# A transformer trunk on one core: cross attentions reordered head by head, expert outputs combined through a 0/1 matrix in two rounded halves, the router's stretch reordered, and 60 extra transposes on TensorE

## What is computed

```
def memory_cross_attention(h, mem_n, wq, wkv, wo):          # 4 heads of 256
    s = einsum('blhd,bmhd->bhlm', q, k) * 256 ** -0.5
    o = einsum('bhlm,bmhd->blhd', softmax(s), v)
    return o @ wo

def moe_swiglu(h, router_w, w_gate, w_up, w_down):
    top_v, top_i = lax.top_k(t @ router_w, 2)
    gates = sum(one_hot(top_i, 8) * softmax(top_v)[..., None], axis=1)
    for e in range(8):
        out = out + gates[:, e:e + 1] * swiglu(t, w_gate[e], w_up[e], w_down[e])
```

## Time and profile before

| | |
|---|---|
| runs | 1725.4, 1728.24, 1728.98 us |
| the profiled execution's own time | 1726.68 us |
| its span, first to last instruction | 1724.9 us |
| TensorE busy | 1673.4 us (97%) |
| VectorE, ScalarE, GpSimd busy | 1297.6 us, 1039.2 us, 21.0 us |
| mean granted TensorE clock | 0.985 of full speed |
| read from HBM | 459.7 MB, 267 GB/s over the span |
| expert passes, 716 to 1718 us | 8 |

### The profile page before, as it was taken

The page is one execution under the profiler, slowest core; times in us unless marked ns, Lnnn a source line. Parts: engine busy times, 40 slices in busy tenths (PEclk is TensorE's granted clock), DMA queues, the critical chain, the costliest instruction groups (busy, mean ns, idle before and its releaser), DMA issues.

```text
span 1724.9 us, 23270 instructions
## 1 busy us (share of the span) xinstructions
PE 1673.4 (97%) x8662; PEld 1419.5 (82%) x8662; DVE 1297.6 (75%) x1120; ACT 1039.2 (60%) x935; POOL 21.0 (1%) x32
## 2 busy tenths in 40 slices
PE   6999999999999999699999999999999999999997
PEld 5997879999887797688888888888788788788785
DVE  6783645555467764698888888888888988988886
ACT  5341435444356544577677677677677677677674
POOL 1000000000000100000000000000000000000000
PEclk9996999999999999899999999999999999999999
DMA  8651525655654445499899899999879999999992
GB/s 314 200 190 50 176 93 171 196 174 192 195 172 137 132 147 198 150 369 370 323 365 372 315 380 359 322 370 372 324 277 365 325 366 349 340 375 342 346 371 120
DMA packets 222435, 461.44 MB, mean 268 GB/s; under 512 B 7314, under 2 KB 52580, under 8 KB 222388
## 3 DMA queue, kind: packets, MB, share of 16 engines
q1 hardware_dynamic: 221696, 459.53, 75.0%
q0 software_dynamic: 528, 1.22, 0.2%
q10 hardware_dynamic: 164, 0.04, 0.0%
HBM read 459.72 MB, written 1.05 MB: 267 GB/s over the span
## 4 chain that ended last, share of the span: by engine, by line
issue 60%; PE 35%; DVE 3%; ACT 1%; DMA 0%; POOL 0%; ACTq 0%; DVEq 0%; POOLq 0%
PE ps L1518 14%; PE ps L1504 8%; PE ps L1743 4%; PE ps L1666 3%; PE ps L1627 1%; PE ps L1594 1%; PE ps L1613 1%; PE ps L1584 1%; DVE w_lo L368 1%; PE ps L1692 0%; ACT w_hi L364 0%; ACT a_hi L542 0%; DMA rows<-in_ev_conv_w 0%; DVE a_lo L879 0%; DVE u L1035 0%
## 5 line engine op out<-in xcount | busy, mean ns | idle before, releaser
L368 DVE TENSOR_TENSOR w_lo<-raw,w_hi 128x2048 fp32r<-128x2048 f32 x431 | 981.8, 2290 | 248.2 <-ACT w_hi L364 246.8
L364 ACT ACTIVATE w_hi<-raw 128x2048 fp32r<-128x2048 f32 x431 | 826.8, 1919 | 364.5 <-PE ps L1893 138.1
L1893 PE MATMUL ps<-w_hi,e_hi 128*128 128x512 f32 x896 | 354.2, 395 | 3.1 <-DVE e_lo L1369 3.1
L1893 PE MATMUL ps<-w_hi,e_lo 128*128 128x512 f32 x896 | 349.6, 390 | 0.0
L1893 PE MATMUL ps<-w_lo,e_hi 128*128 128x512 f32 x896 | 349.0, 389 | 0.0
L1893 PEld LDWEIGHTS ps<-w_hi,e_hi 128*128 128x128 f32 x896 | 168.3, 188 | 36.5 <-issue 3.3
L1893 PEld LDWEIGHTS ps<-w_hi,e_lo 128*128 128x128 f32 x896 | 168.2, 188 | 35.8
L1893 PEld LDWEIGHTS ps<-w_lo,e_hi 128*128 128x128 f32 x896 | 168.4, 188 | 33.6
L1915 PE MATMUL ps<-w_hi,at_hi 128*128 128x512 f32 x448 | 175.0, 391 | 1.9 <-DVE at_lo L1381 1.9
L1915 PE MATMUL ps<-w_hi,at_lo 128*128 128x512 f32 x448 | 174.4, 389 | 0.0
L1915 PE MATMUL ps<-w_lo,at_hi 128*128 128x512 f32 x448 | 174.3, 389 | 0.0
(11 more groups left out here) (294 smaller groups left out, 1816.0 us busy)
## 6 DMA issues: line engine op xcount, KB each, us to landing
raw<-in_moe_w_up SPq DMA_DIRECT2D x112, 1024.0 KB, 6.9
raw<-in_moe_w_gate SPq DMA_DIRECT2D x110, 1024.0 KB, 7.0
raw<-in_moe_w_down SPq DMA_DIRECT2D x110, 1024.0 KB, 6.1
raw<-in_xa_wkv SPq DMA_DIRECT2D x16, 1024.0 KB, 5.1
raw<-in_ev_w_in SPq DMA_DIRECT2D x14, 1024.0 KB, 8.7
raw<-in_od_w_in SPq DMA_DIRECT2D x12, 1024.0 KB, 5.0
raw<-in_ffd_w_gate SPq DMA_DIRECT2D x11, 1024.0 KB, 5.4
raw<-in_ffd_w_up SPq DMA_DIRECT2D x11, 1024.0 KB, 5.3
```

The source lines that it names most:

```text
L364: nc.scalar.activation(w_hi[:, n % CUT, :], at_, ACT.Copy).then_inc(hi_cut, 1)
L368: nc.vector.tensor_tensor(w_lo[:, n % CUT, :], place(n, r, behind)[0], w_hi[:, n % CUT, :].bitcast(F32), ALU.subtract).then_inc(lo_cut, 1)
L1893: mm = T.matmul(ps[:, bank, :], s, m, start=(h == 0 and k == 0 and j == 0), stop=(h == 1 and k == 3 and j == 2))
```

## The change

Four parts.

1. **Cross attentions by heads.** The scores, the transposes and the values of a head are put between the slabs of wq and wo. wo is taken with both column halves of its upper rows first, then of its lower rows, so that its first slabs need only heads 0 and 1. The banks are by kind: scores in 4 and 5 by turns, transposes in 6, values in 7. ACT and DVE get their order written out, slab cuts in between.
2. **0/1 combine.** `spread` is the transpose of `pack` itself, float32r. y is written as `y_hi` (ACT) and `y_lo` (DVE), both float32r, and `combine` is two matmuls for each of the four pieces. The gate is multiplied in where DVE adds to X. `pgate` goes.
3. **The router's stretch.** Some slab cuts, the calculation of the gates, the load of ACT's Silu table and the waits for the table of passes change places; the opening of the first pass is taken out in front of the loop. The entries behind 8 of the table are made with 5 operations in place of 11.
4. **60 transposes** of the identity into PSUM bank 3: 4 after the router's product, 24 before the counting matmuls, 20 before the gather, 12 after it.

```
-            slabs[f"o{i}"] = t_all(kpn(xa_wo[i]))
+            slabs[f"o{i}"] = [t_slab(kpn(xa_wo[i]), 512 * b)[h] for h in range(2) for b in range(2)]
 # ACT, cross
-                stage(f"q{i}", 4)
-                for h in range(XH): (exp of each head)
-                for h in range(XH): (xa_pt of each head)
-                for h in range(XH): (a_hi of each head)
-                stage(f"o{i}", 4 if i == 0 else 3)
+                cut(0) ; cut(1) ; cut(2) ; exps(0) ; cut(3) ; turned(0) ; exps(1) ; head_hi(0) ; turned(1)
+                exps(2) ; head_hi(1) ; exps(3) ; cut(4) ; turned(2) ; head_hi(2) ; turned(3) ; cut(5)
+                head_hi(3) ; cut(6)
+                if i == 0:
+                    cut(7)
 # DVE, cross
+                cut(0) ; q_got(0) ; cut(1) ; q_got(1) ; top(0) ; cut(2) ; shares(0) ; q_got(2) ; top(1)
+                cut(3) ; shares(1) ; q_got(3) ; head_lo(0) ; top(2) ; top(3) ; shares(2) ; head_lo(1)
+                shares(3) ; cut(4) ; head_lo(2) ; cut(5) ; head_lo(3) ; cut(6)
+                dve.wait_ge(slab_used, FIRST[f"o{i}"] + 3)
+                x_event(0, f"o{i}")()
 # TensorE, cross
+                q_slab(0) ; q_slab(1) ; scores(0) ; q_slab(2) ; scores(1) ; turn_p(0) ; q_slab(3)
+                values(0) ; scores(2) ; turn_p(1) ; scores(3) ; values(1)
+                o_slab(0, 0, {2: lambda: turn_p(2)})
+                values(2) ; turn_p(3)
+                o_slab(1, 0, {2: lambda: values(3)})
+                o_slab(0, 1, {})
+                o_slab(1, 1, {2: lambda: turn_x(0)} if i == 1 else {})
 # ACT, router and passes
+            cut_hi(act, G0 + 1)
             for h in range(2):
                 act.wait_ge(acc_free, BANKS["o1"] + 2 * h + 2)
...
-            cut_hi(act, G0 + 1)
+            cut_hi(act, G0 + 2)
             act.wait_ge(n_rstd, NORMS["moe"] + 1)
...
-            cut_hi(act, G0 + 2)
             act.wait_ge(r_m, 1)
             nc.scalar.activation(lg[:, 9, 2:4], lg[:, 9, 0:2], ACT.Exp).then_inc(r_e, 1)
-            act.wait_ge(r_tab, 1)
-            n_pass = act.value_load(table[0:1, 0:1], min_val=NE, max_val=NE + 3)
             nc.scalar.activation(mx[:, 0:1], ident[:, 0:1], ACT.Silu).then_inc(g_sig, 1)
...
+            def y_up(q):
+                act.wait_ge(slab_used, G0 + PASS + PASS * q)
+                nc.scalar.activation(y_hi[:, :], ps[:, 2:4, :].rearrange("p a n -> p (a n)"),
+                                     ACT.Copy).then_inc(y_top, 1)
 # a_next: cut G0, pack_hi, cut G0+1, y_up(q - 1), then cuts G0+2 to G0+5
 # DVE, router and passes
-            stage("o1", 3, {1: x_event(0, "o1"), 2: lambda: turn_lo("moe", a_hi, a_lo, tiles=range(4))})
+            cut_lo(dve, G0 + 1)
+            turn_lo("moe", a_hi, a_lo, tiles=range(4))
...
-            cut_lo(dve, G0 + 1)
             dve.wait_ge(r_lt, 1)
             V.tensor_copy(logits[:, :], ps[0:NE, LOGITS, 0:256]).then_inc(r_ls, 1)
...
             V.tensor_tensor(mask, one1, one2, ALU.add).then_inc(r_cnt, 1)
+            cut_lo(dve, G0 + 2)
             dve.wait_ge(r_ps, 2)
 # the gates (L1317 to L1325 before) now come behind pack_lo(0) and the cuts of G0+3 to G0+5
             def v_y(q):
-                dve.wait_ge(slab_used, G0 + PASS + PASS * q)
-                V.tensor_copy(y[:, :], ps[:, 2:4, :]...).then_inc(y_sb, 1)
+                dve.wait_ge(y_top, q + 1)
+                V.tensor_tensor(y_lo[:, :], ps[:, 2:4, :]..., y_hi[:, :]..., ALU.subtract).then_inc(y_sb, 1)
 # add_pass
-                    V.tensor_tensor(X[:, t, :], ps[...], X[:, t, :], ALU.add)
+                    V.scalar_tensor_tensor(out=X[:, t, :], in0=ps[...], scalar=gate16[:, t, bass.ds(col, 1)],
+                                           in1=X[:, t, :], op0=ALU.mult, op1=ALU.add)
 # TensorE, router and passes
+            def keep_going(n):
+                for _ in range(n):
+                    T.transpose(ps[:, 3, 0:P], ident, ident)
+            keep_going(4)
             pe.wait_ge(r_ls, 1)
...
+            keep_going(24)
             pe.wait_ge(r_cnt, 1)
...
+            keep_going(20)
...
-                        mm = T.matmul(ps[:, b0 + o, :], spread[:, t * P:(t + 1) * P], y[:, 512 * o:512 * o + 512],
-                                      start=True, stop=True)
+                        for yv in (y_hi, y_lo):
+                            mm = T.matmul(ps[:, b0 + o, :], spread[:, t * P:(t + 1) * P],
+                                          yv[:, 512 * o:512 * o + 512], start=yv is y_hi, stop=yv is y_lo)
...
             gather(0)
+            keep_going(12)
+            opening(0)
             pe.wait_ge(r_tab, 1)
```

More of the change, by code:

```diff
@@ L150, in trunk_kernel @@
         ta = sb("ta", [P, 2048])
+        with ExitStack() as s:
+            sb("tb_front", [P, D], F32, s)
+            y_lo = sb("y_lo", [P, D], F32R, s)
         tb = sb("tb", [P, 2048])
@@ L820, in a_next @@
                 pack_hi(q)
-                for n in range(1, 6):
+                cut_hi(act, G0 + 1, 7 * q, behind)
+                y_up(q - 1)
+                for n in range(2, 6):
                     cut_hi(act, G0 + n, 7 * q, behind)
@@ L1343, in _ @@
             pack_tokens(0)
-            over, incl, rk, hit = (row16[:, i, 0:8] for i in range(4))
+            over, incl, rk = (row16[:, i, 0:8] for i in range(3))
             link(V.tensor_scalar(over, ps[0:1, 1, 16:24], float(BLK), None, ALU.is_gt))
@@ L1484, in room, with slab_t, gemm_t @@
                     pe.wait_ge(acc_free, upto - 4)
-            def gemm_t(name, blocks, hi, lo, base=None, before_last=None):
+            def slab_t(n, bank, h, hi, lo, before_k=None):
+                slab_ready(n)
+                wh, wl = (shaped(w[:, n % CUT, :], 4) for w in (w_hi, w_lo))
+                for k in range(4):
+                    if before_k is not None:
+                        before_k(k)
+                    for t in range(2):
+                        ah, al = (a[:, 4 * h + k, t * P:(t + 1) * P] for a in (hi, lo))
+                        for j, (s, m) in enumerate(cuts(ah, al, wh[:, k, :], wl[:, k, :])):
+                            mm = T.matmul(ps[:, (bank + t) % 4, :], s, m, start=(h == 0 and k == 0 and j == 0),
+                                          stop=(h == 1 and k == 3 and j == 2))
+                mm.then_inc(slab_used, 1)
+            def gemm_t(name, blocks, hi, lo, base=None):
                 for b in range(blocks):
@@ new lines, in cross @@
+                q_slab(0)
+                q_slab(1)
+                scores(0)
+                q_slab(2)
+                scores(1)
+                turn_p(0)
+                q_slab(3)
+                values(0)
+                scores(2)
+                turn_p(1)
+                scores(3)
+                values(1)
+                o_slab(0, 0, {2: lambda: turn_p(2)})
+                values(2)
+                turn_p(3)
+                o_slab(1, 0, {2: lambda: values(3)})
+                o_slab(0, 1, {})
@@ L1932, in _, with opening @@
             gather(0)
-            pe.wait_ge(r_tab, 1)
-            n_pass = pe.value_load(table[0:1, 0:1], min_val=NE, max_val=NE + 3)
-            with pe.Fori(0, n_pass) as q:
+            def opening(q):
                 pe.wait_ge(e_l, q + 1)
@@ L1943, in _ @@
                 half_in(G0 + 3, i, 1, 1)
+            keep_going(12)
+            opening(0)
+            pe.wait_ge(r_tab, 1)
+            n_pass = pe.value_load(table[0:1, 0:1], min_val=NE, max_val=NE + 3)
+            with pe.Fori(0, n_pass) as q:
                 with pe.If(q > 0):
+                    opening(q)
                     combine(q - 1)
-                pe.wait_ge(pg_rdy, q + 1)
                 for t in range(2):
-                    mm = T.transpose(ps[:, 5, t * P:(t + 1) * P], pgate[:, t, :], ident)
+                    mm = T.transpose(ps[:, 5, t * P:(t + 1) * P], pack[:, t, :], ident)
                 mm.then_inc(pg_ps, 1)
```

196 lines of the change are left out of this document (123 added, 73 removed).

## The result

Before: 1727.51 us, median of 4 runs (1725.4 to 1728.98). Changed: **1708.32 us**, median of 4 (1707.91 to 1708.48). Ratio 0.9889, 95% interval 0.9872 to 0.9907. The profiled execution of the changed kernel has an own time of 1708.24 us and a span of 1706.4, so 18.5 us of span less than the one of before.

| stretch of the span | before, us | after, us | difference | forecast |
|---|---|---|---|---|
| start to wq of cross attention 0 | 202.77 | 204.46 | +1.7 | 0 |
| wq to the end of wo, cross attention 0 | 66.8 | 60.9 | -5.9 | -5.2 |
| between | 353.6 | 353.6 | 0 | 0 |
| wq to the router's product, cross attention 1 | 67.3 | 68.4 | +1.1 | +2.4 |
| router's product to G0 | 25.7 | 19.0 | -6.7 | -5.6 |

The account below looks back on a forecast made before the run. TensorE was taken to bound the kernel, its instructions setting each expert pass. Cross attention 0 -5.2, cross attention 1 with the router's stretch -3.2 and passes -9.1 sum to -17.5 us: forecast 1709.5 us, range 1702 to 1718.

Parts of the forecast that it names:

- Cross attention 0: From wq to the end of wo: softmax beside slabs removes 5.8 us of waits and half clock, less 0.6: -5.2 us.
- ten changes between kinds of matmul: In cross attention 0: some ten more switches between matmul kinds may cost 0.1 us each, 0.6 taken.
- Cross attention 1: Late G0 load leaves 5.3 us idle in wo's last slab, eating the gain: +0.4, plus +2 for half clock.
- Router's stretch: From wo's end to the first matmul of G0: reordered cuts, full-clock gather, transposes and earlier Silu table load: -5.6 us.
- The 20 transposes: Before the gather: they take 2.1 us where TensorE waited 1.8 for `pack`: +0.3 us.
- beside the counting: 0: Router's stretch: DVE's 2.3 us cut of G0+2 runs beside the counting's five pairs, costing 0.
- Passes: Expert passes: seven at -1.4 us each, first pass +0.8 to 1, end -0.3; together -9.1 us.
- The wait at G0+6 of the first pass: First expert pass: the gates' seven operations ahead of DVE's cut, less `pgate`, cost +0.8 to 1 us.
- The first rival: Router's stretch: transposes don't hold the clock, so it falls during the wait for the pick: 1713 us, chance 0.25.
- G0 isn't what wo waits for: Cross attention 1: values 3 or loads come earlier, so it gains 5.3 us without half clock: 1702 us, chance 0.1.
- Cuts fall behind in every pass: Expert passes: y's chain through ACT and DVE makes TensorE wait 1 us, not 0.2: 1715 us, chance 0.12.
- The ring of loads runs dry: Expert passes: loads limit; at 340 GB/s a pass takes 129.5 us: 1755 us total, chance 0.03.

Follow-up runs that it names:

- experiment 1: Changed kernel with the loads of G0 to G0+3 issued before the wait for values 3 of cross attention 1: 1700.12 us.
- experiment 2: Changed kernel with VectorE's first addition to X put ahead of its cut of G0 in cross attention 1: 1706.21 us.
- experiment 11: The kernel of experiment 9 without any of the change's 60 transposes: 1688.29 us.
- experiment 5: Changed kernel with the gates' seven operations moved on VectorE ahead of the cuts of G0+3 to G0+5: 1706.64 us.
- experiment 3: Changed kernel without its 60 transposes of the identity: 1709.87 us.
- experiment 4: Changed kernel with 42 more transposes of the identity ahead of turn_x(0) in cross attention 1, G0's load still late: 1705.89 us.
- experiment 9: Changed kernel with G0's loads early, gates early, and added transposes ahead of mem's turn, in the retention and ahead of the last combine: 1684.9 us.
- experiment 6: Changed kernel with the old float32 combine: y copied by VectorE, one float32 matmul per half bank: 1718.63 us.
- experiment 12: Kernel before with only the two cross attentions by heads, wo's new slab order and their cuts, softmax and additions: 1724.93 us.
- experiment 7: Changed kernel with 13 more transposes of the identity in the retention, ahead of the first head's values: 1695.92 us.
- experiment 10: The kernel of experiment 9 with the change's 60 transposes cut down to the 24 ahead of the counting: 1688.63 us.
- experiment 8: Changed kernel with G0's loads early, gates early, 13 transposes ahead of mem's turn and 18 ahead of the last combine: 1699.4 us, one execution 1685.13.

## Why the prediction was right, point by point

- **Total.** 1709.5 forecast, 1708.3 measured. The parts of the change made 20.2 us where 17.5 were counted; the profile's start gave 1.7 back. The two errors are opposed, so that the sum came within 1.2 us is partly luck. (Added up straight, the ends of the parts give 1705.5 to 1715.7, not 1706 to 1714.)
- **Cross attention 0**, -5.2 against -5.9: right in mechanism. The 0.6 for ten changes between kinds of matmul was the mis-sized term: they cost nothing, the chain adds up from 1.73, 0.44 and the slabs.
- **Cross attention 1**, +2.4 against +1.1. Its idle time was forecast at 5.3 us with the chain that it has, and measured at 5.14; experiment 1 shows the cause, experiment 2 that the chain's last link was not it. The half clock behind it was forecast at 2 us; 68.4 less 61.6 less 5.1 leaves 1.7. The largest part of the difference is again the changes between kinds of matmul, 0.8 us here, which cost nothing: values 3 end 47.3 us behind wq's start instead of 47.9, and the load goes out with them.
- **Router's stretch**, -5.6 against -6.7. From the router's product to the logits' copy 9.3 us became 5.6: -3.7 (forecast -3.4). From there to the gather 7.7 became 7.2: -0.5, where +0.3 was forecast. Two terms were mis-sized. The 20 transposes were priced against a wait of 1.8 us, but `pack` itself is ready at 700.05, 0.1 us ahead of their end: +0.1 and not +0.3. And "beside the counting: 0" left out what full clock is worth there: from the first counting matmul to the gather it is 3.53 us, 3.82 in experiment 11, where all five pairs run at half clock (0.43 us apart instead of 0.22), and 4.07 before. The last 0.2 is a wait of 0.22 us that DVE had inside the calculation of `pack` and has no longer. From gather to G0 8.7 became 6.2: -2.5, as forecast.
- **Passes**, -9.1 against -8.7. Combine -1.6, as forecast. The wait at G0+2 forecast at 0.2 is 0.1 or less, so a pass gained 1.5, not 1.4. The wait at G0+6 of the first pass was forecast at 0.8 to 1 and is 1.34, from the gates' operations (experiment 5). The end was forecast at -0.3 and came out at +0.1: TensorE waits 2.37 us for `y_lo` and the clock falls within the last combine (0.63 us for its last matmuls), which the prediction did not look for.
- **The first rival**, that transposes don't hold the clock, falls. It was drawn from the fall around 236 us, where groups of four transposes stand between waits, and held back by a wait of 3 us seeming too short against one of 4.22. Both readings were wrong. Ahead of those transposes stood a wait of 1.70 us (to 234.81), and in the changed kernel the same groups of four stand in cross attention 0 without a wait and without a fall. The wait of 2.92 us is enough for a fall (experiment 3), and the transposes prevent it. The clock stayed at 1.00 through 24 and 20 transposes in the router's stretch, fell without them (experiments 3 and 11), and stayed through 42 in a row (experiment 4). The Trainium skill (TensorE: Matmul & The Clock Gate, Part 4: PE-mode transpose) says that full clock does not engage for transposes, since they don't count as busy in the same way. For these ones (float32, 128x128 by the identity) the trace disagrees, and the measurement decides. That they also raise a clock at half is read from durations alone: the first 16 transposes of the kernel, behind two tiny matmuls, take 3.34 us in the changed kernel and 3.65 before, so the last ones were faster.
- **G0 isn't what wo waits for**: it was (experiment 1). **Cuts fall behind in every pass**: no wait at G0+2 or G0+6 after the first pass. **The ring of loads runs dry**: DMA share 0.98 at 357 GB/s, no wait for a load. With the version of experiment 9, whose passes have the same length, the same holds.

What decides whether the clock falls at 33 us is settled in part by the length of the wait. Ten profiles are of kernels without transposes ahead of the turn of mem. In four of them (the kernel before, experiments 1, 2 and 3) the first slab starts at half speed (0.63 us a matmul until 21 to 22 us), the wait is 1.3 to 1.5 us, and the clock stays. In the other six the first slab is at full speed and the wait is 3.1 us; four of these fall (the changed kernel, experiments 4, 6 and 12), two do not (5 and 7). What decides between these, and behind the waits of 1.5 to 1.9 us elsewhere, stays open: the retention's 1.5 us brought the clock down in nine of ten profiles, the 1.9 us for `at_lo` in two of fourteen (experiments 2 and 4). That the four timed runs of the changed kernel all fell at 33 us, as their spread of 0.6 us, their equal mean clock of 0.987 and experiment 1 suggest, is argued, not shown.

## What to carry to other kernels

A reordering that closes one wait brings the next one forward: follow the first load behind the reordered stretch to the wait that holds its issue, for it was late before and nobody asked for it. Read the granted clock over the whole span, not only around the change: here a wait of 1.5 us ahead of a stretch of small matmuls cost 12 us, more than the change took out of all the passes. Where TensorE must wait for 1.5 us or more, transposes of the identity into a free bank held its clock here. In the router's stretch it was not enough to fill the longest wait (experiment 10), and filling only pays where work follows that the half clock would slow down.

## What the runs showed of the hardware

- Behind waits as short as 1.5 us (retention) and 2.25 us (experiment 10) TensorE's clock went to half, in most executions but not in all: 1 of 6 kept it in experiment 8, and 1 of 5 in experiment 10 was 2.1 us below the next. The time of one kernel so takes two values, 1685 and 1699 us in experiment 8.
- At half clock a stream of small matmuls with TensorE busy in every microsecond (88 recorded from 131 to 156 us) did not bring the clock back; the same stream at full clock (86 in 14 us) did not lose it.
- Half clock behind the same idle time of 5.1 to 5.4 us lasted 3.4 us in the changed kernel and 6.8 us in those of experiments 3 and 5, though all three are the same program up to there. The Trainium skill (TensorE: Matmul & The Clock Gate, Part 1) says that the ramp differs from run to run of one kernel; the profiles agree. On top of the idle time it cost 1.7 us in the changed kernel and 2.8 in experiment 3 (69.7 from wq to the router's product, less 61.6, less 5.3).
- The windows give the clock as 1.00 from the start of every profile, yet matmuls of 128x512 take 0.63 us in the kernel before from 18.8 to 21.3 us, as they do elsewhere at 0.50, and 0.39 from 21.7 on. In the first 20 us the durations tell the clock, the windows do not.
